# A hybrid decoder step: the row projections with the tokens' activations stationary, and gv's group ahead of gq and gk

## The reference

```
def project_inputs(xn, pos, w_in, q_g, k_g, kidx_g, gla_wa2, gla_ba):
    h = xn @ w_in                                  # 1024 -> sum(IN_SPLITS)
    q, k, v, qi, ki, wi, gq, gk, gv, ga, gr, gate_a, gate_b = jnp.split(h, offs, axis=-1)
    q = partial_rope(rms_norm(q.reshape(B, T, N_HEADS, HEAD_DIM), q_g), pos, ROT_DIM)
    k = partial_rope(rms_norm(k.reshape(B, T, N_KV_HEADS, HEAD_DIM), k_g), pos, ROT_DIM)
    qi = partial_rope(qi.reshape(B, T, IDX_HEADS, IDX_DIM), pos, IDX_ROT_DIM)
    ki = partial_rope(rms_norm(ki, kidx_g)[:, :, None, :], pos, IDX_ROT_DIM)[:, :, 0, :]
    log_a = jax.nn.log_sigmoid((ga @ gla_wa2 + gla_ba).astype(jnp.float32)) / GLA_TAU
...
    # dsa_attention: I[t,s] = sum_h wi[t,h] relu(qi[t,h].ki[s]), top-k keys of each query, softmax over them
    # gla_recurrence: gated linear attention, chunks of 64 tokens, with gq, gk, gv, log_a
...
    g_out = rms_norm(gla_o, gla_on_g).reshape(B, T, GLA_V_W) * jax.nn.silu(gr)
    merged = jax.nn.sigmoid(gate_a) * (attn_o @ w_oa) + jax.nn.sigmoid(gate_b) * (g_out @ w_ob)
```

## Time and profile before

| | |
|---|---|
| runs | 1836.33 us median of 3 (1833.85 to 1837.96) |
| profiled execution | span 1837.1 us, 34,731 instructions; what lies around the span is not shown, so its own time is taken to be the span |
| PE busy | 1764.5 us, 96%, 13,422 matmuls |
| DVE, ACT, POOL busy | 1090.8, 793.2, 785.9 us |
| PE's clock | the granted clock reads 9 (90% or more of full speed) in each 40th of the span |
| DMA | 151.53 MB, mean 82 GB/s |

### The profile page before, as it was taken

How to read it: one execution, slowest core, us unless ns; L and a number is a source line. 1 busy time by engine, 2 the same in 40 slices (tenths; PEclk the granted TensorE clock), 3 DMA queues, 4 the chain that set the end, 5 groups by cost and what they waited for, 6 DMA issues and landing times.

```text
span 1837.1 us, 34731 instructions
## 1 busy us (share of the span) xinstructions
PE 1764.5 (96%) x13422; PEld 1685.4 (92%) x13422; DVE 1090.8 (59%) x2154; ACT 793.2 (43%) x1515; POOL 785.9 (43%) x508
## 2 busy tenths in 40 slices
PE   7998999999999999999999999999999999999998
PEld 7997888788999999999999878877899999999998
DVE  4655786355587537637536658744556874474463
ACT  4443214465466426426433422145645663363352
POOL 2322443342447447536333333425234563574452
PEclk9999999999999999999999999999999999999999
DMA  5232225214223413313222222342143234233122
GB/s 154 70 87 58 52 73 143 70 36 115 81 81 93 115 58 102 110 50 87 61 70 70 72 74 60 82 126 60 44 119 104 59 93 115 69 94 104 51 63 78
DMA packets 285711, 151.53 MB, mean 82 GB/s; under 512 B 17831, under 2 KB 284139, under 8 KB 285547
## 3 DMA queue, kind: packets, MB, share of 16 engines
q1 hardware_dynamic: 285546, 149.30, 29.7%
HBM read 141.89 MB, written 7.37 MB: 81 GB/s over the span
## 4 chain that ended last, share of the span: by engine, by line
PE 75%; DVE 15%; issue 3%; ACT 3%; SPq 2%; DMA 1%; POOL 0%; DVEq 0%; ACTq 0%; POOLq 0%
PE prod L1352 41%; PE prod L1406 8%; PE prod L1408 8%; PE prod L1407 8%; DVE scores L2710 2%; DVE top L2708 1%; PE aux L1765 1%; PE aux L1753 1%; PE aux L1465 1%; SPq L1179 1%; DVE in_lo L2247 1%; SPq L1185 1%; PE aux L1526 1%; PE aux L1728 1%; DVE aux L2480 1%
## 5 line engine op out<-in xcount | busy, mean ns | idle before, releaser
L1790 POOL TENSOR_TENSOR w_lo<-w_raw,w_hi 128x1024 fp32r<-128x1024 f32 (+1 forms) x158 | 370.8, 2347 | 757.6 <-ACT w_hi L1889 753.1
L1352 PE MATMUL prod<-in_hi,w_hi 128*128 128x288 f32 x1504 | 345.0, 311 | 12.8 <-DVE in_lo L2247 7.8
L1352 PE MATMUL prod<-in_lo,w_hi 128*128 128x288 f32 x1504 | 327.4, 300 | 0.0
L1352 PE MATMUL prod<-in_hi,w_lo 128*128 128x288 f32 x1504 | 326.1, 299 | 0.0
L1352 PEld LDWEIGHTS prod<-in_hi,w_hi 128*128 128x128 f32 x1504 | 244.8, 193 | 33.0 <-issue 24.6
L1889 ACT ACTIVATE w_hi<-w_raw 128x1024 fp32r<-128x1024 f32 (+1 forms) x158 | 163.1, 1032 | 246.1 <-PE prod L1352 245.8
L1352 PEld LDWEIGHTS prod<-in_lo,w_hi 128*128 128x128 f32 x1504 | 247.4, 193 | 0.0
L1352 PEld LDWEIGHTS prod<-in_hi,w_lo 128*128 128x128 f32 x1504 | 247.2, 192 | 0.0
L1406 PE MATMUL prod<-t_hi,ff_hi 128*128 128x288 f32 x704 | 208.7, 296 | 1.5 <-ACT in_sum L1941 0.7
L1352 PE MATMUL prod<-mid_hi,w_hi 128*128 128x288 f32 x960 | 207.6, 298 | 2.0 <-DVE mid_lo L2247 2.0
L1407 PE MATMUL prod<-t_lo,ff_hi 128*128 128x288 f32 x704 | 207.8, 295 | 0.0
(11 more groups left out here) (316 smaller groups left out, 3213.5 us busy)
## 6 DMA issues: line engine op xcount, KB each, us to landing
w_raw<-in_w_in SPq DMA_DIRECT2D x76, 512.0 KB, 3.8
ff_gate<-in_w_ffn_gu SPq DMA_DIRECT2D x44, 512.0 KB, 5.2
ff_up<-in_w_ffn_gu SPq DMA_DIRECT2D x44, 512.0 KB, 4.0
w_raw<-in_w_ffn_down SPq DMA_DIRECT2D x32, 512.0 KB, 4.1
w_raw<-in_w_o SPq DMA_DIRECT2D x16, 512.0 KB, 3.9
w_raw<-in_w_ffn_down SPq DMA_DIRECT2D x16, 384.0 KB, 3.4
k_pages<-in_cache_k SPq DMA_DIRECT2D x32, 128.0 KB, 2.0
v_pages<-in_cache_v SPq DMA_DIRECT2D x32, 128.0 KB, 2.0
```

The lines of the kernel that those rows point to most:

```text
L1352: ins = e.matmul(slot(g)[:, h, :], w[:, slot_w, i * P:(i + 1) * P], a[:, i, h * HALF:(h + 1) * HALF], start=first, stop=last)
L1790: e.tensor_tensor(w_lo[:, p % 2, 0:n], w_raw[:, p % RAW_RING, 0:n], w_hi[:, p % 2, 0:n].bitcast(F32), ALU.subtract).then_inc(w_lo_done, 1)
```

## The change

The layer's list of steps is changed, and the way in which 15 of its panels are computed.

- q, k with v, qi with ki, wi and ga, and gv become four *row groups* (rq, rkv, rqi, rgv) of 512, 512, 340 and 512 columns. Each is still loaded in four panels, but a panel now holds two k-tiles with all the group's columns. On PE a part is one tile of 128 tokens in one k-tile: the activations are stationary and the weights move, three matmuls (row_part, L1393 to L1395). With the fourth token tile come two matmuls for the samples (L1406, L1408), whose stationary operand s_both holds the high and the low part of their 64 tokens side by side. A group's sums fill all four prod banks and one aux bank. So the rows come out as they are wanted.
- ACT's stage copies, PE's transposes and DVE's scalings of rows go. In their place DVE evicts token tiles 0 and 1 and ACT tiles 2 and 3, with r_rows as factor, and the samples' two halves are added (ACT copies one to stage, DVE adds and scales). s_both takes a small ACT copy and a small DVE operation in each k-tile.
- ga now lies in rows, and is turned back for the decay (step gaT: five small transposes, two copies by DVE).
- rgv's group stands ahead of gq and gk. The norms of q's rows go into rkv's panels, k's into rqi's, ki's into rgv's.
- The first three gr panels (INDEX_PANELS = 3) are woven with the index items, where gv's four were. GLA_PANELS counts from gr and becomes 12: nine panels (the last gr, eight gta) are woven with the GLA, and eight (gtb) with the attention.
- At the start the first panel's load goes behind the second x tile, and ACT's squares (step xstat) behind the copy of the second panel's weights. rstd of the first norm comes after the second panel.

```
-GLA_PANELS = 10
+INDEX_PANELS = 3
+GLA_PANELS = 12
...
+ROW_PARTS = {"rq": [(O_Q, ATTN_W, 0)], "rkv": [(O_K, 2 * KV_W, 0)],
+             "rqi": [(O_QI, IDX_ROW_W + IDX_HEADS, 0), (O_GA, RANK, IDX_ROW_W + IDX_HEADS)],
+             "rgv": [(O_GV, GV_W, 0)]}
...
+    def rows(kind):
+        return [(kind, i, [("w_in", 2 * i * P, 2, off, w, place) for off, w, place in ROW_PARTS[kind]])
+                for i in range(4)]
+
+    out += rows("rq") + rows("rkv") + rows("rqi") + rows("rgv")
...
         for p in range(base, first["gq"]):
             self.start(p)
+            if p == 0:
+                self.add("xstat")
             for i in range(KD):
                 self.add("part", p, i)
-                if i == 0 and p > base:
-                    self.row(p - 1)
-                if first["k"] <= p < first["qi"] + 1 and i in (3, 6) and len(normed) > NTILE:
+                due = 2 * NTILE if p < first["rqi"] else NTILE if p < first["rgv"] else 0
+                if p >= first["rkv"] and i in (2, 6) and len(normed) > due:
                     self.extra_step(normed.pop(0)[0])
-            if p == base:
+            if p == base + 1:
                 self.rstd(1)
...
-        self.woven(range(first["gq"], first["gv"]), items)
+        items = [[], [("gaT",), ("qn_end",)], [("z",)], [("z_min",)], [("qkT", 0)], [("decay",)], [("decay_ref",)],
+                 [("qkT", 1)], [("decay_exp",), ("qkT", 2)], [("qkT", 3)], [("qkT", 4)]]
+        self.woven(range(first["gq"], first["gr"]), items)
...
-        self.woven(range(first["gv"], first["gr"]), items)
+        self.woven(range(first["gr"], first["gr"] + INDEX_PANELS), items)
...
-        self.woven(range(first["gr"], split), items)
+        self.woven(range(first["gr"] + INDEX_PANELS, split), items)
...
             for t in range(NTILE):
...
-                if t == 3:
+                if t == 0:
                     load_gains(0)
-            for p in range(RAW_RING):
+                if t == 1:
+                    load_panel(0)
+            for p in range(1, RAW_RING):
                 load_panel(p)
...
+                def row_part(p, i):
+
+                    kind, idx, _ = PANELS[p]
+                    t, kt, width = i % 4, 2 * idx + i // 4, ROW_W[kind]
...
+                    if first and g >= 2:
+                        if PANELS[p - 1][0] in ROWS:
+                            e.wait_ge(rows_out[t], row_no(kind) - 1)
...
+                    e.matmul(out, in_hi[:, kt, tok], hi_w, start=first, stop=False)
+                    e.matmul(out, in_hi[:, kt, tok], lo_w, start=False, stop=False)
+                    ins = e.matmul(out, in_lo[:, kt, tok], hi_w, start=False, stop=last)
+                    if last:
+                        ins.then_inc(row_ready[t], 1)
+                    if t < 3:
+                        return
...
+                    e.matmul(aux[:, bank(key), 0:width], s_both[:, kt, :], hi_w, start=first, stop=False,
+                             skip_group_check=True)
+                    ins = e.matmul(aux[0:NS, bank(key), 0:width], s_both[:, kt, 0:NS], lo_w, start=False,
+                                   stop=last, skip_group_check=True)
...
+                            for t in (2, 3):
+                                e.wait_ge(row_ready[t], row_no(kind_p))
+                                for src, dst in row_dests(kind_p, t):
+                                    ins = e.activation(dst, src(row_bank(p, t)), ACT.Copy, scale=r_rows[:, t:t + 1])
+                                ins.then_inc(rows_out[t], 1)
...
+                            for t in (0, 1):
+                                e.wait_ge(row_ready[t], row_no(kind_p))
+                                for ps, dst in row_dests(kind_p, t):
+                                    ins = e.tensor_scalar(dst, ps(row_bank(p, t)), r_rows[:, t:t + 1], None, ALU.mult)
+                                ins.then_inc(rows_out[t], 1)
```

More of the change, by code:

```diff
@@ L157, in const_array @@
     return c
+ROW_PARTS = {"rq": [(O_Q, ATTN_W, 0)], "rkv": [(O_K, 2 * KV_W, 0)],
+             "rqi": [(O_QI, IDX_ROW_W + IDX_HEADS, 0), (O_GA, RANK, IDX_ROW_W + IDX_HEADS)],
+             "rgv": [(O_GV, GV_W, 0)]}
+ROW_W = {kind: sum(w for _, w, _ in parts) for kind, parts in ROW_PARTS.items()}
+ROWS = tuple(ROW_PARTS)
 def make_panels():
     out = []
[L164 to L169, removed]
+    def rows(kind):
+        return [(kind, i, [("w_in", 2 * i * P, 2, off, w, place) for off, w, place in ROW_PARTS[kind]])
+                for i in range(4)]
+    out += rows("rq") + rows("rkv") + rows("rqi") + rows("rgv")
+    for kind, off, n in (("gq", O_GQ, 2), ("gk", O_GK, 2), ("gr", O_GR, 4), ("gta", O_GTA, 8), ("gtb", O_GTB, 8)):
         out += [(kind, i, [("w_in", 0, KD, off + i * P, P, 0)]) for i in range(n)]
@@ L193, with panel_cols @@
     RAW_READY.append(_count[_p % RAW_RING])
+def panel_cols(p):
+    kind, idx, parts = PANELS[p]
+    return 2 * ROW_W[kind] if kind in ROWS else sum(part[2] for part in parts) * P
 SMALL_LOADS = 5
@@ L274, in start @@
     def start(self, p):
-        for g in self.groups[p]:
-            self.open(("g", g), 4 + g % 2)
+        kind, idx, _ = PANELS[p]
+        if kind not in ROWS:
+            for g in self.groups[p]:
+                self.open(("g", g), 4 + g % 2)
+        elif idx == 0:
+            self.open(("rs", kind), 3)
         self.weights(p + 1)
@@ L594, in extra_step @@
         kind = step[0]
+        if kind == "gaT":
+            for i in range(2):
+                self.open(("gaT", i), i)
         if kind == "z":
@@ L882, in build @@
         ln_done = semaphore("ln_done")
-        ga_done = semaphore("ga_done")
+        sample_hi = semaphore("sample_hi")
+        sample_lo = semaphore("sample_lo")
+        row_ready = [semaphore(f"row{t}_ready") for t in range(4)]
+        row_part_done = semaphore("row_part_done")
+        rows_out = [semaphore(f"rows{t}_out") for t in range(NTILE)]
         decay_done = semaphore("decay_done")
@@ L930, in build @@
             layer = p // N_LAYER
-            for g in plan.groups[p]:
+            for n, g in enumerate(plan.groups[p]):
                 if kind == "o":
                     free_of["g", g] = (x_added, layer * X_ADDS + idx + 1)
-                elif kind in STAGED:
-                    free_of["g", g] = (staged, plan.stage_use[layer, ("row", p)] + 1)
+                elif kind in ROWS:
+                    free_of["g", g] = (rows_out[2 * n + 1], layer * len(ROWS) + ROWS.index(kind) + 1)
                 elif kind == "down":
@@ L1886, in copy_w @@
                     if p >= 2:
[L1887 to L1888 removed]
+                        e.wait_ge(*panel_done(p - 2))
+                    n = panel_cols(p)
                     e.activation(w_hi[:, p % 2, 0:n], w_raw[:, p % RAW_RING, 0:n], ACT.Copy).then_inc(w_hi_done, 1)
@@ L2004, in body @@
                                      scale=gains[:, layer, gain:gain + 1]).then_inc(split_hi, 1)
+                        if norm == 1:
+                            e.activation(s_both[:, kt, 0:NS], x_t[:, kt, SEQ:NT], ACT.Copy,
+                                         scale=gains[:, layer, gain:gain + 1]).then_inc(sample_hi, 1)
                     elif kind == "rstd" and layer == 0 and step[1] == 1:
@@ L2048, in body @@
                         if t == 0:
-                            last = last_panel({"q": "q", "k": "k", "x": "misc"}[part])
-                            for row in ("rowX", "rowY"):
-                                e.wait_ge(free((row, last)), emptied((row, last)))
+                            for t2 in range(NTILE):
+                                e.wait_ge(rows_out[t2], row_no({"q": "rq", "k": "rkv", "x": "rqi"}[part]))
                         if u_all:
```

250 lines of the change are left out of this document (131 added, 119 removed).

## The result

The changed kernel takes 1852.70 us (median of 4 runs, 1852.19 to 1857.36) against 1836.09 (4 runs): a ratio of 1.0092, 95% interval 1.0079 to 1.0106. It is 16.6 us slower, where 11.4 us faster was forecast, and outside the range (1807 to 1846; the forecast's own 1816 to 1834).

The account below looks back on a forecast made before the run. TensorE, busy for 96% of the span, was taken to bound the kernel through its queue and waits. Layer 0 summed to -4.9 us, layer 1 to -6.5, together -11.4: 1836.3 to 1825 us, own range 1816 to 1834, with rivals 1807 to 1846.

Parts of the forecast that it names:

- The price of 512 columns: Row projections: a matmul with 512 moving columns takes 0.23 us, so a group of 112 takes 25.8 us.
- the start: Layer 0 before the first panel matmul: PE starts at about 18.1 instead of 18.86, -0.8 us, bounds -3 and +2.
- The banks are short: Rival, row groups' ends: all four product banks used, evictions 1 us late at eight ends, 8 us, 1833; chance 0.05.
- The 340-column group: Row projections: 112 matmuls at 0.156 us, 17.5 us a layer, with POOL's 1.6 us lowering fitting into a 4.4 us panel.
- Attention stage. Two of ten panels go ... a fifth of it is -8.9: Attention, each layer: a fifth of 44.2 us panel time on the chain goes; a quarter given back leaves -6.5 us.
- The cache pages' loads stay as they are: Attention stage: page loads unchanged, with 11.8% of the chain being SP's issuing of them.
- The cover was needed: Rival, woven stages: other engines already set the pace, 8 us a layer returned, not 19.6; 1848 us; chance 0.15.
- Index stage ... Sum -5.6: Index stage, each layer: fewer panel parts -5.9, three turns -2.6, gr's closings +2.9; bounds -9 and -2.
- The clock falls oftener: Rival, thin places: PE's granted clock drops four more times a layer, 1.7 us each, about 1837 us; chance 0.08.
- GLA stage ... Sum -7.5: GLA stage, each layer: closings and table load -8.4, gta multiplications +2.3, panel -1.8, turn -0.8, third closing +1.2; bounds -9, -3.
- One panel of ten goes: -1.8: GLA stage: one panel fewer returns 10% of the 17.3% panel share of 99.7 us, -1.8 us a layer.
- gq and gk: Stage behind the projections: loses misc's turn and 0.9 us idle, gains five ga turns and a copy, -0.9 us a layer.

Follow-up runs that it names:

- parts left out: Changed kernel with six of eight parts left out in every second gtb panel, four panels a layer, in the attention stage: 1853.60 us, ratio 1.0097.
- the filled run: Changed kernel with 27 unused 512-column matmuls a layer put on TensorE where it waits in the index stage: 1848.04 us, ratio 1.0069.

## Why the prediction was wrong

- *The price of 512 columns, the banks, the start.* Right: 0.23 us, 25.5 to 25.7 us a group behind the first of a layer, -0.3 us at the start for a forecast -0.8. "The banks are short" did not come about: in its row groups PE waits for no eviction.
- *The 340-column group.* Mis-sized by 2.4 us a layer. The prediction checked POOL's 1.6 us against the panel's 4.4, but not what stands ahead of the weight copy in ACT's queue. The norms that were moved into these panels stand there, and wait for DVE.
- *"Attention stage. Two of ten panels go ... a fifth of it is -8.9", less a quarter.* This is the step that failed by most: 11.4 us over both layers. It took panel time on the chain of waits for time that goes when the panel goes. The chain names the one that arrives last, and right behind PE stood the heads' loop: the last eleven heads took 28 us with 95, 77 or 47 panel matmuls, and with parts left out the stage did not shorten. The step also says "The cache pages' loads stay as they are". They came 1.2 us behind the start of the stage, and PE waited 3.5 and 3.4 us for them in place of 0.5 and 1.3; that is at most 3.0 and 2.1 us of the 6.1 and 5.3 that are missing a layer.
- *The rival "The cover was needed"* had this mechanism (8 us a layer returned; 8.9 and 8.7 measured) and 1848; with the 340-column group's 4.8 us it would have been at 1853. Its sum is right partly by luck: it also counted on ACT's pace in the index stage, where it was the clock.
- *"Index stage ... Sum -5.6".* Off by 9.4 us over both layers. The term's count was right: it gives 43.6 and 42.1 us, and with the clock at 1.00 and 0.96 the same panels took 42.3 and 43.8 (the filled run), 9.0 us less than in the changed kernel. What it had at nothing is the fall of the clock. The rival "The clock falls oftener" expected windows of 5 us at 1.7 us each (eight of them on 1825 make 1838.6, not its 1837); here one fall lasted. From 168.3 to 180.3 the granted clock is 0.50 with PE busy for 11.37 of 12.00 us:

```profile
168.30:180.30 12.00, 11.37 (x39) 8.62 (x38) 4.58 (x9) 4.02 (x8) 0.00 (x0) 0.50 0.41 102
```

- *"GLA stage ... Sum -7.5".* Right in size (-6.5 and -7.7). That it was the DVE steps that went is read from the chain of the earlier trace rows; no run tests them alone. "One panel of ten goes: -1.8" was hardly there to have: up to the pages' issue the stage takes 95 to 96 us with nine panels, with eight and with seven.
- *gq and gk:* -0.9 forecast, -0.6 and +0.8 measured.

One small product of the first sum is off as well: ten statistic matmuls of 110 ns are 1.1 us, not 0.9.

The chances carried the same mistake. They gave 0.15 to the cover and 0.08 to the clock as if they were apart. Both came with fewer panels where PE waits, and arrived together.

## What to carry to other kernels

Work that fills another loop's waits is worth its time only down to that loop's own pace. Before moving it out, leave some of it out and look whether the stage shortens, and compare stretches of the same granted clock; a stage whose busy share is near 90% with two further engines in a loop beside it may already be at its floor. And if filler must move, move what sits in straight stretches in its place: here the cheaper form of the products pays a little (0.9964), and the order that came with it does not.

## What the runs showed of the hardware

- A slow clock can last through work, and how long differs between executions of the same code. In the changed kernel PE stood at 0.50 for 12 us with only 0.6 us of idle in it, in a stretch whose index products alternate with panel parts. Just before, PE had waited 2.2 us for DVE and 0.4 us for ACT. With the same code and the same two waits in front, the run with parts left out has pairs of panel matmuls 0.48 us apart up to 171.1 us, and 0.27 from 174.9 on. With 6.2 us of further matmuls in the waits the stage's clock was 1.00 and 0.96, and the stage 5.0 and 4.0 us shorter. The Trainium skill (TensorE: Matmul & The Clock Gate, Part 1) has idle bring the clock down and steady work bring it up; the fall agrees with that here, but what kept it down through this work no run tells.
- The granted clock's record can miss a stretch. At the first row group the row says 1.00, and 12 matmuls take 4.98 us, 0.43 from start to start; from 24 us on they stand 0.23 apart:

```profile
18.52:23.50 4.98, 4.98 (x12) 3.92 (x13) 4.98 (x12) 4.98 (x12) 0.00 (x0) 1.00 0.17 65
```

That is about half the pace, the pace of the lower level (1.2 GHz). In the kernel before, the first 5.00 us of the same start hold 21 matmuls of 288 columns, 0.24 us each in place of 0.133, and are recorded at 0.50. So the loss here (4.98 - 12 x 0.23 = 2.2 us) is in no clock column.
